# Hybrid mixer of a fused two-block network: convolution chunks first, taps redistributed, mask by TensorE, gates by tanh

## What is computed

```python
def stick_breaking_attention(q, k, v):
    ...
        z = jnp.einsum('bhqd,bhkd->bhqk', q_blk, k).astype(jnp.float32) * scale
        earlier = key_pos[None, :] < query_pos[:, None]
        log_keep = jnp.where(earlier, jax.nn.log_sigmoid(-z), 0.0)
        log_stick = lax.cumsum(log_keep, axis=3, reverse=True) - log_keep
        w = jnp.where(earlier, jnp.exp(jax.nn.log_sigmoid(z) + log_stick), 0.0)
        return jnp.einsum('bhqk,bhkd->bhqd', w.astype(v.dtype), v)

def conformer_conv(u_glu, conv_w, conv_b, ln_g, ln_b):
    a, g = jnp.split(u_glu, 2, axis=-1)
    u = a * jax.nn.sigmoid(g)
    y = lax.conv_general_dilated(
        u, conv_w[:, None, :], window_strides=(1,),
        padding=[(CONV_WIDTH - 1, 0)],
        dimension_numbers=('NWC', 'WIO', 'NWC'),
        feature_group_count=CONV_CHANNELS) + conv_b
    yf = y.astype(jnp.float32)
    mu = jnp.mean(yf, axis=-1, keepdims=True)
    var = jnp.mean(jnp.square(yf - mu), axis=-1, keepdims=True)
    yn = (yf - mu) * lax.rsqrt(var + NORM_EPS) * ln_g.astype(jnp.float32) + ln_b.astype(jnp.float32)
    return jax.nn.silu(yn).astype(u.dtype)

def hybrid_mixer(h, w_in, conv_w, conv_b, conv_ln_g, conv_ln_b,
                 gla_w_alpha, gla_b_alpha, gla_norm_g, w_branch, w_out):
    proj = h @ w_in
    ...
    branches = jnp.stack([sb_out, conv_out, gla_out], axis=2)
    branch_d = jnp.einsum('bsgw,gwd->bsgd', branches, w_branch)
    gates = jax.nn.sigmoid(gate_logits.reshape(b, s, N_BRANCHES, D_MODEL))
    merged = jnp.sum(gates * branch_d, axis=2)
    return merged @ w_out
```

## Time and profile before

| | |
|---|---|
| median of 3 runs | 2132.66 us (2131.63 to 2134.47) |
| profiled execution | 2131.91 us |
| its span | 2130.1 us |
| PE busy | 2076.7 us, 97% of the span |
| DVE busy | 1325.1 us, 62% |
| ACT busy | 1141.4 us, 54% |
| chain that ended last, by engine | PE 81%, DVE 11%, ACT 5% |
| DMA | 370.16 MB, mean 174 GB/s |

### The profile page before, as it was taken

How to read it: one execution, slowest core, us unless ns; L and a number is a source line. 1 busy time by engine, 2 the same in 40 slices (tenths; PEclk the granted TensorE clock), 3 DMA queues, 4 the chain that set the end, 5 groups by cost and what they waited for, 6 DMA issues and landing times.

```text
span 2130.1 us, 24559 instructions
## 1 busy us (share of the span) xinstructions
PE 2076.7 (97%) x9974; PEld 1704.5 (80%) x9974; DVE 1325.1 (62%) x1659; ACT 1141.4 (54%) x1412; POOL 0.2 (0%) x4
## 2 busy tenths in 40 slices
PE   7999999899999999999999999999999999999998
PEld 6888887778888888887778888778888887888887
DVE  6555589775546546589775556766554567666554
ACT  6445666664446445656563446656634466566443
POOL 0000000000000000000000000000000000000000
PEclk9999999999999999999999999999999999999999
DMA  7554653465555554643465555434455554435553
GB/s 262 184 193 146 213 171 126 158 202 174 193 183 189 196 179 157 209 164 120 159 216 178 189 167 193 158 133 155 155 191 185 171 193 139 152 135 183 182 192 104
DMA packets 243857, 370.16 MB, mean 174 GB/s; under 512 B 15952, under 2 KB 151456, under 8 KB 243744
## 3 DMA queue, kind: packets, MB, share of 16 engines
q1 hardware_dynamic: 239360, 355.71, 49.9%
q10 hardware_dynamic: 4384, 12.88, 1.7%
HBM read 367.50 MB, written 1.05 MB: 173 GB/s over the span
## 4 chain that ended last, share of the span: by engine, by line
PE 81%; DVE 11%; ACT 5%; issue 2%; DMA 1%; SPq 0%; ACTq 0%; DVEq 0%
PE ps L522 74%; DVE w_lo L1770 3%; DVE scratch L1983 2%; ACT w_hi L1199 2%; PE ps L628 1%; PE ps L611 1%; PE ps L588 1%; PE ps L1140 1%; PE ps L1121 1%; DMA raw<-in_ffn_w_up 1%; DVE x L1811 1%; PE ps L670 1%; DVE scratch L2019 0%; DVE scratch L2023 0%; DVE scratch L2031 0%
## 5 line engine op out<-in xcount | busy, mean ns | idle before, releaser
L1770 DVE TENSOR_TENSOR w_lo<-raw,w_hi 128x2048 fp32r<-128x2048 f32 x342 | 773.6, 2267 | 424.3 <-ACT w_hi L1199 423.6
L1199 ACT ACTIVATE w_hi<-raw 128x2048 fp32r<-128x2048 f32 x342 | 647.9, 1895 | 342.8 <-PE ps L522 295.6
L522 PE MATMUL ps<-w_hi,hT_hi 128*128 128x512 f32 x2000 | 797.2, 399 | 2.2 <-DVE w_lo L1770 2.2
L522 PE MATMUL ps<-w_lo,hT_hi 128*128 128x512 f32 x2000 | 780.7, 390 | 0.0
L522 PE MATMUL ps<-w_hi,hT_lo 128*128 128x512 f32 x2000 | 759.1, 391 | 0.0
L522 PEld LDWEIGHTS ps<-w_hi,hT_hi 128*128 128x128 f32 x2000 | 376.8, 188 | 84.2 <-issue 6.4
L522 PEld LDWEIGHTS ps<-w_hi,hT_lo 128*128 128x128 f32 x2000 | 375.4, 188 | 80.1
L522 PEld LDWEIGHTS ps<-w_lo,hT_hi 128*128 128x128 f32 x2000 | 377.2, 189 | 73.8
L522 PE MATMUL ps<-w_hi,bT_hi 128*128 128x512 f32 x704 | 278.1, 395 | 4.7 <-DVE bT_lo L2006 4.7
L522 PE MATMUL ps<-w_hi,bT_lo 128*128 128x512 f32 x704 | 275.2, 391 | 0.0
L522 PE MATMUL ps<-w_lo,bT_hi 128*128 128x512 f32 x704 | 275.1, 391 | 0.0
(11 more groups left out here) (288 smaller groups left out, 1166.2 us busy)
## 6 DMA issues: line engine op xcount, KB each, us to landing
raw<-in_w_in SPq DMA_DIRECT2D x160, 512.0 KB, 4.5
raw<-in_ffn_w_gate SPq DMA_DIRECT2D x88, 512.0 KB, 3.7
raw<-in_ffn_w_up SPq DMA_DIRECT2D x88, 512.0 KB, 4.7
raw<-in_ffn_w_down SPq DMA_DIRECT2D x88, 512.0 KB, 4.2
raw<-in_w_gate SPq DMA_DIRECT2D x44, 512.0 KB, 3.7
raw<-in_w_up SPq DMA_DIRECT2D x44, 512.0 KB, 4.7
raw<-in_w_down SPq DMA_DIRECT2D x44, 512.0 KB, 4.2
raw<-in_w_out SPq DMA_DIRECT2D x32, 512.0 KB, 4.4
```

Source lines behind the costliest of these rows:

```text
L522: mm = nc.tensor.matmul(bank(t, half), act[:, tiles[i], t * P:(t + 1) * P], w, start=start and (i, n) == steps[0], stop=stop and (i, n) == ...
L1199: nc.scalar.activation(w_hi[:, u % HIGH_RING, cols], raw[:, slot, cols], ACT.Copy).then_inc(high_ready, 1)
L1770: V.tensor_tensor(w_lo[:, slot, cols], raw[:, slot, cols], flat(w_hi[:, u % HIGH_RING, cols]), ALU.subtract).then_inc(low_ready, 1)
```

## The change

- The chunk order starts with the convolution's two pieces. Its gate times input product, its transposition and the first taps move ahead of the gated linear attention; 15 taps (before: 10) now lie between the chunk units and 16 (before: 21) in section units 0 to 9, alternately two and one.
- The causal mask is no longer applied by two DVE instructions per pair of heads. PE adds it to the logits as one more product, identity by a mask tile in reduced format, for each head. DVE copies the two tiles `sb_ident` and `sb_bar` once, in the first FFN.
- DVE's `sb_keep` is split: `sb_copy(c)` (logits to SBUF, once the absolute value has been taken) at the head of iteration 2c+1, and `sb_softplus(c)`, from that copy, at the end of iteration 2c+1. `sb_exponent(c)` goes from iteration 2c+1 to the head of iteration 2c+2. `merge` goes to the head of the following iteration.
- `sb_sums` has two products instead of three for each head: the columns 0 to 384 in one.
- Sigmoids of the gates and of the convolution's gate become Tanh of half the argument; the 1 is added in the multiplication on DVE, and the factor one half is put into later copies.
- `conv_rows` goes to after unit 10 and `conv_normed` to after unit 12, with DVE's centring in iteration 11 ahead of `weight_low`, and ACT's part moved likewise.

```diff
-A_CHUNKS = {"gla_qk": 2560, "gla_v": 3072, "gla_r": 3584, "conv_a": 1536, "conv_g": 2048,
+A_CHUNKS = {"conv_a": 1536, "conv_g": 2048, "gla_qk": 2560, "gla_v": 3072, "gla_r": 3584,
             "sb_q": 0, "sb_k": 512, "sb_v": 1024}
...
@@ PE sb_logits
-                nc.tensor.matmul(ps[:, 4 + e, 0:256], sbkT[r, c, 0:P], sbqT[r, c, :], start=True, stop=True)
+                nc.tensor.matmul(ps[:, 4 + e, 0:256], sbkT[r, c, 0:P], sbqT[r, c, :], start=True, stop=False)
...
+            for e, r in heads:
+                barred = ps[:, 4 + e, 0:384].rearrange("p (b n) -> p b n", b=3)[:, 0::2, :]
+                mm = nc.tensor.matmul(barred, sb_ident[:, :], sb_bar[:, :].unsqueeze(1).broadcast_to([P, 2, P]),
+                                      start=False, stop=True)
@@ PE sb_sums
-            pe.wait_ge(*after("sb_keep", f"masked{c}", l))
+            pe.wait_ge(*after("sb_keep", f"softplus{c}", l))
...
-                nc.tensor.matmul(ps[:, 6 + e, 256:384], konst("tri_ge"), s[:, 256:384], start=True, stop=True)
-                nc.tensor.matmul(ps[:, 6 + e, 0:256], konst("tri_ge"), s[:, 0:256], start=True, stop=False)
+                nc.tensor.matmul(ps[:, 6 + e, 0:384], konst("tri_ge"), s, start=True, stop=False)
                 mm = nc.tensor.matmul(ps[:, 6 + e, P:256], konst("ones"), s[:, 256:384], start=False, stop=True)
@@ PE mixer_a
-            steps = {("gla_v", 1): [gla_alpha], ("gla_r", 1): [gla_decays],
-                     ("conv_a", 1): [gla_updates], ("conv_g", 1): [gla_reads], ("sb_q", 0): [conv_turn],
+            steps = {("conv_g", 1): [gla_alpha], ("gla_qk", 0): [conv_turn], ("gla_v", 0): [gla_decays],
+                     ("gla_r", 0): [gla_updates], ("sb_q", 0): [gla_reads],
                      ("sb_k", 0): [sb_turn_q], ("sb_k", 1): [gla_turn], ("sb_v", 0): [sb_turn_k]}
...
-                        if n == 13:
+                        if n == 12:
                             conv_normed(l)
...
-                    if n == 11:
+                    if n == 10:
                         conv_rows(l)
@@ ACT
+            scale = rstd_half if func == ACT.Tanh else rstd_in
...
-                            rows(sg[:, half, :, :], chunk_rows(half), "gates", f"gate{i}_{half}", ACT.Sigmoid)
+                            rows(sg[:, half, :, :], chunk_rows(half), "gates", f"gate{i}_{half}", ACT.Tanh)
@@ DVE
-        def sb_keep(l, c):
+        def sb_copy(l, c):
+
+            dve.wait_ge(*after("sb_weights", f"abs{c}", l))
+            V.tensor_copy(pair_of_heads(sb_z), ps[:, 4:6, 0:384]).then_inc(*done("sb_keep", f"copied{c}"))
+
+        def sb_softplus(l, c):
 
             dve.wait_ge(*after("sb_weights", f"ln{c}", l))
-            pair_of_heads = lambda w: w.rearrange("p (e n) -> p e n", e=2)
-            V.scalar_tensor_tensor(pair_of_heads(sb_sp), ps[:, 4:6, 0:384], 0.0, pair_of_heads(sb_e), ALU.max,
-                                   ALU.add).then_inc(*done("sb_keep", f"softplus{c}"))
-            dve.wait_ge(*after("sb_keep", f"softplus{c}", l))
-            V.tensor_tensor(diagonal(sb_sp), diagonal(sb_sp), mask("sb_keep"), ALU.mult).then_inc(*done("sb_keep", f"masked{c}"))
-            V.tensor_copy(pair_of_heads(sb_z), ps[:, 4:6, 0:384]).then_inc(*done("sb_keep", f"copied{c}"))
             dve.wait_ge(*after("sb_keep", f"copied{c}", l))
-            V.tensor_tensor(diagonal(sb_z), diagonal(sb_z), mask("sb_neg"), ALU.add).then_inc(*done("sb_keep", f"barred{c}"))
+            V.scalar_tensor_tensor(sb_sp, sb_z, 0.0, sb_e, ALU.max, ALU.add).then_inc(*done("sb_keep", f"softplus{c}"))
...
             for n in range(18):
-                i, m = n // 6, n % 6
+                if n in (2, 4, 6, 8):
+                    sb_exponent(l, n // 2 - 1)
+                if n in (1, 3, 5, 7):
+                    sb_copy(l, n // 2)
+                if n in (3, 5, 7, 9):
+                    sb_low(l, n // 2 - 1)
+                if n and (n - 1) % 6 >= 4:
+                    merge(L, k + n - 1, (n - 1) // 6, (n - 1) % 6 - 4)
+                if n == 11:
+                    conv_centre(l)
                 weight_low(L, k + n + AHEAD)
...
+                if n < 10:
+                    taps(2 if n % 2 == 0 or n == 9 else 1)
+                if n in (1, 3, 5, 7):
+                    sb_softplus(l, n // 2)
+                if n == 11:
+                    conv_normed(l)
+                if n == 14:
                     conv_low(l)
```

More of the change, by code:

```diff
@@ L686, in gla_decays @@
             pe.wait_ge(*after("gla_in", "qk", l))
+            pe.wait_ge(*after("conv_glu", "u", l))
             for c in range(2):
@@ L736, in conv_turn @@
             pe.wait_ge(*after("conv_glu", "glu", l))
+            pe.wait_ge(*after("gla_keep", "logits", l))
             turn(conv_u, 6).then_inc(*done("conv_turned", "u"))
@@ L805, in conv_normed @@
             pe.wait_ge(*after("conv_norm", "normed1", l))
-            pe.wait_ge(*after("sb_keep", "copied3", l))
+            pe.wait_ge(*after("sb_keep", "exponent3", l))
             turn(conv_n, 4).then_inc(*done("conv_normed", "turned"))
@@ L1411, in merged_high @@
                                      ps[:, 4 + 2 * kh + t, :].rearrange("p (c n) -> p c n", c=4),
-                                     ACT.Copy).then_inc(*done("merged_high", f"k{kh}t{t}"))
+                                     ACT.Copy, scale=0.5).then_inc(*done("merged_high", f"k{kh}t{t}"))
         def mixer_a(L):
@@ L1417, in mixer_a @@
                     "gla_r": (gr, "gla_in", "r", ACT.Silu), "conv_a": (conv_u, "conv_in", "a", ACT.Copy),
-                    "conv_g": (conv_s, "conv_in", "g", ACT.Sigmoid), "sb_q": (sb_q, "sb_in", "q", ACT.Copy),
+                    "conv_g": (conv_s, "conv_in", "g", ACT.Tanh), "sb_q": (sb_q, "sb_in", "q", ACT.Copy),
                     "sb_k": (sb_k, "sb_in", "k", ACT.Copy), "sb_v": (sbv, "sb_in", "v", ACT.Copy)}
@@ L1426, in mixer_a @@
                     rms_ready(L, 1)
-                if name == "gla_r":
+                if name == "conv_g":
+                    act.wait_ge(*after("tanh_scale", "half", l))
+                if name == "gla_qk":
                     gla_alpha(l)
-                if name == "conv_a":
+                if name == "gla_v":
                     gla_decays(l)
                 if name == "sb_k":
+                    gla_std(l)
                     act.wait_ge(*after("sb_turned", "q", l))
@@ L1468, in mixer_a @@
                     section_step(l, 6 * i + 4 + half)
+                    if (i, half) == (1, 1):
+                        conv_std(l)
                     k += 1
@@ L1868, in ffn @@
                 dve.wait_ge(const_loaded, 16 * 4)
+                V.tensor_copy(sb_ident[:, :], ident).then_inc(*done("start", "ident"))
+                V.tensor_copy(sb_bar[:, :], konst("sb_neg")).then_inc(*done("start", "bar"))
                 rope_angles()
@@ L1964, in conv_glu @@
             dve.wait_ge(*after("conv_in", "g", l))
-            V.tensor_tensor(conv_u, conv_u, conv_s, ALU.mult).then_inc(*done("conv_glu", "glu"))
+            V.scalar_tensor_tensor(conv_u, conv_s, 1.0, conv_u, ALU.add, ALU.mult).then_inc(*done("conv_glu", "glu"))
         def conv_in(l):
             dve.wait_ge(*after("conv_turned", "u", l))
-            V.tensor_copy(uT[:, :, CPAD:CPAD + T], two(6)).then_inc(*done("conv_glu", "u"))
+            V.tensor_scalar(uT[:, :, CPAD:CPAD + T], two(6), 0.5, None, ALU.mult).then_inc(*done("conv_glu", "u"))
             dve.wait_ge(*after("conv_glu", "u", l))
@@ L2045, in merge @@
             if i == 0:
-                V.tensor_tensor(out_, rows, ps[:, 2 * half:2 * half + 2, :], ALU.mult).then_inc(*done("merge", f"branch{i}_{half}"))
+                V.scalar_tensor_tensor(out_, rows, 1.0, ps[:, 2 * half:2 * half + 2, :], ALU.add, ALU.mult).then_inc(*done("merge", f"branch{i}_{half}"))
                 return
-            V.tensor_tensor(rows, rows, ps[:, 2 * half:2 * half + 2, :], ALU.mult).then_inc(*done("merge", f"gated{i}_{half}"))
+            V.scalar_tensor_tensor(rows, rows, 1.0, ps[:, 2 * half:2 * half + 2, :], ALU.add, ALU.mult).then_inc(*done("merge", f"gated{i}_{half}"))
             dve.wait_ge(*after("merge", f"gated{i}_{half}", l))
@@ L2055, in merged_low, with taps @@
                 tiles = (slice(None), slice(4 * kh, 4 * kh + 4), slice(t * P, (t + 1) * P))
-                V.tensor_tensor(hT_lo[tiles], ps[:, 4 + 2 * kh + t, :].rearrange("p (c n) -> p c n", c=4),
-                                flat(hT_hi[tiles]), ALU.subtract).then_inc(*done("merged_low", f"k{kh}t{t}"))
+                V.scalar_tensor_tensor(hT_lo[tiles], ps[:, 4 + 2 * kh + t, :].rearrange("p (c n) -> p c n", c=4), 0.5,
+                                       flat(hT_hi[tiles]), ALU.mult, ALU.subtract).then_inc(*done("merged_low", f"k{kh}t{t}"))
         def mixer_a(L):
             l, k = L.l, U_FFN
+            tap = [0]
+            def taps(count):
+                conv_taps(l, tap[0], tap[0] + count - 1)
+                tap[0] += count
```

(22 more changed lines are left out.)

64 lines of the change are left out of this document (30 added, 34 removed).

## The result

The changed kernel takes 2163.28 us (median of 4 runs, 2161.6 to 2165.29) against 2132.14 us before (4 runs). The ratio is 1.0144, with a 95% interval of 1.0127 to 1.0162: 1.4% slower. The forecast was 2159.5 us in a range of 2146 to 2170.

The account below looks back on a forecast made before the run. PE was taken to bound the chunk stage, with waits leaving holes in the section. On 2131.9 us, + 20.7 - 7.7 = 13.0 and + 20.7 - 6.1 = 14.6 gave 2159.5 us, range 2146 to 2170.

Parts of the forecast that it names:

- Where PE waits: Section of each mixer: PE's sb_sums waits four times for DVE's softplus, near 5 us each; earlier waits go.
- The chain: Section: softplus queues behind tap and low part, which waits for ACT's high part; sums to sums 21.7 us, sb_out 20.7 later.
- The mask product: PE's path and ACT's chain, once per pair of heads: 0.3 us, bounded between 0 and 0.9.
- The clock: PE behind each new softplus wait: a stretch at lower clock costing 1.6 us, eight times, 12.8 us in all.
- The tail: End of each mixer: waits for the last tap and before unit 16 go; 7.7 us back in the first, 6.1 second.
- Parts at nothing: More taps in the chunk stage, Tanh for Sigmoid, added 1 and halves, two constants: no time; under 2 us per mixer if uncovered.
- the rival that hung on one table set for both: ACT's chain: no table load between Exp and Ln, cycle 1.28 us shorter, 8 times; 2149.3 us, chance 0.03.
- The first rival: Section: softplus is in time, named waits go and no new one comes; 2109.7 us, chance 0.07.

Follow-up runs that it names:

- the mended kernel: Changed kernel with DVE's softplus moved ahead of weight_low and the tap in iterations 1, 3, 5 and 7: 2105.69 us, ratio to before 0.9874.

## Why the prediction was right

**Where PE waits: right.** It named the mechanism, the place and the number: four waits per mixer, near 5 us; there are four of 5.0 to 5.1, and no other. The experiments that cut its links, one by one, gave 19.6 us (tap), 33.8 us (high part) and 57.6 us (both and the low part).

**The chain: right to 0.1 us.** The first sums were put at 321.3 on before's time axis. They start at 322.85, and the mixer starts 1.45 later: 321.4. From `sb_out`'s start to the next sums the sum gave 7.86 + 0.03 + 2.21 + 1.58 + 0.97 + 0.03 = 12.68. The window between is 333.10 to 345.79, 12.69. The mask product, which no row of before had, was put at 0.3:

```profile
310.90 0.70 PE L765 MATMUL ps<-scratch 64*128 64x256 f32 x4
...
311.75 0.50 PE L772 MATMUL ps<-sb_bar,sb_ident 128*128 128x256 f32 x2
312.10 0.39 PE L523 MATMUL ps<-w_hi,hT_hi 128*128 128x512 f32 x1
```

From the logits to the next unit it is 1.20 us where it was 0.86 (309.45 to 310.31), so 0.34. The estimate from the page "TensorE: Matmul & The Clock Gate" of the Trainium skill, section "Wait — 56ns, not 53.3ns?", was 0.22 us; the trace shows 0.35 (311.75 to 312.10), and the measurement decides.

**The clock: the term that was too small.** It was 1.6 us for each wait, read from the slow units after waits of 2.1 and 2.3 us. By the medians, filling the waits gave back 16.4 us, 2.05 each. In the windows from the sums to the next `sb_out` it varies:

```profile
322.85:333.10 10.25, 10.25 (x32) 7.51 (x32) 3.72 (x4) 2.65 (x2) 0.00 (x0) 0.71 0.01 2
...
390.34:399.38 9.04, 9.04 (x33) 6.57 (x33) 2.67 (x2) 2.65 (x2) 0.00 (x0) 0.82 0.01 2
```

With the waits filled the same way takes 7.4 us (322.80 to 330.20), so these two lose 2.9 and 1.6. All eight lose 17.8 us in the trace, 2.2 each. From sums to sums it is therefore 22.9, 21.8 and 22.8 us in the first mixer, where the prediction had 21.7, and the attention stretches grow by 23.2 and 23.4 us in place of 20.7. The forecast came as near as it did because only this term was off, and because the tail gave back 1.1 us more than it had counted: 23.2 - 8.3 + 23.4 - 6.6 = 31.7 us in the traces, 31.1 between the medians, 27.6 forecast. The range had this in it, by the argument that a wait twice as long may cost more (up to 1.3 us each); the middle of that argument's span, and not its lower end, would have been the better value.

**The tail: right.** 7.7 and 6.1 us were to come back, 8.3 and 6.6 did. (The terms written for the first, 2.1 + 2.3 + 2 x 1.6, add up to 7.6.) That both moves were needed (taps for the one wait, the chain for the other) is shown by the kernel with the tail put back, as far as it goes: the earlier chain without the earlier taps was not run.

**Parts at nothing: right.** The chunk stage kept its 75.9 us with no wait, though DVE has 10.3 us more to do there and not 8, Tanh changed nothing in the changed kernel (0.07 us between the medians), and the load between Exp and Ln stayed (314.07), so the rival that hung on one table set for both fell.

**The first rival** was priced at 2109.7 us. With the order mended it is 2105.7, 4 us less, and its granted clock is 1.000 on average over the span. Nor did all its waits go: 1.6 us per mixer are left. Held against the trace of before, the first mixer is 12.9 us shorter from the first logits to the next block's transposes (priced at 12.5) and the second 11.3 (priced at 9.7). The sum had counted the lower clock only behind the tail's waits, and before's second mixer has such a stretch behind an `sb_out` wait too: from the logits at 994.87 to the next sums it takes 8.0 us, and 6.7 where nothing is slow. The other 2.0 us lie behind the mixers, where before's granted clock is 0.91 in the window 1380:1400 and that of the mended kernel stays at 1.00; the reordering touches nothing there, so this part is chance.

## What to carry to other kernels

On an in-order engine the place of an instruction is a dependency: when a step is moved, ask of every instruction that it now stands behind what that one waits for, and follow that wait into the other engine's queue. An instruction whose result is needed two stages later must not stand ahead of one whose result is needed next if it can block. And parts that pay (here less work on DVE and an earlier tail, 26 us together with the order right) can be hidden behind one line at the wrong place, so before a change is given up, its waits should be read and its order tried.

## What the runs showed of the hardware

- A wait of PE of 2 us can cost clock, and whether it does varies. After waits of 2.1 and 2.3 us the granted clock of the following unit was 0.79 and 0.76. After one of 2.4 us in the second mixer it was 1.00 (the window of the earlier trace rows spans that wait, which ends at 1057.58; the window 1058:1064 is at 1.00 too). With the softplus ahead of the tap, a wait of 3.46 us was followed by no loss (7.41 us from the sums at 341.21 to `sb_out`), and the next one, of 3.46 too, lost 1.7 (9.10 from 359.72).
- After each of the four waits of 5 us in the first mixer the first product of the sums took 1.61 to 1.65 us in place of 0.91 with the waits filled: PE was at the lower level, 1.2 GHz. Such a wait costs about 7 us in the end.
- The clock also falls where the change reaches nothing. Behind a wait for the first low part, near 17.5 us, it was 0.77 in the window 17.5:25 in four of the twelve traces (after a wait of 2.29 us in each) and 1.00 in the other eight (1.38 to 2.25 us). In the changed kernel's trace that moves all that follows by 1.45 us. Differences of 1 to 2 us between two kernels can be this alone.
- Useless products are cheaper than idling, if they fit in the wait: 28 of them, 5.03 us, in place of 5.1 us of waiting brought 2.05 us for each wait, by the medians.
- A softplus of 768 columns takes DVE 0.95 us from SBUF (321.84) and 0.96 from PSUM: the copy to SBUF does not make it faster.
